# Dealing a block's slots out by 4 (rank mod 16) + rank div 16 in a one-core MoE kernel

## The chip, the core and the metric

The kernel runs as one program on one core of a Trainium2 chip. The metric is the device time in microseconds (us). In these texts TensorE is PE, VectorE is DVE, ScalarE is ACT, GpSimd is POOL and SyncE is SP. The core's transfers run on 16 DMA engines; SP's transfers are those of the hardware queue (q1), POOL's those of the software queue (q0).

## The reference

One decoder layer over 512 tokens of width 2048: a norm, an input projection, two recurrent branches, a merge, and then a mixture of experts, which alone matters here. Its core, shortened:

```python
g_sel = jnp.argmax(g_logits, axis=-1)                        # 1 of 4 groups
top_l, top_i = lax.top_k(e_logits, TOP_K_IN_GROUP)           # 2 of 8 experts in it
expert_id = g_sel[:, None] * EXPERTS_PER_GROUP + top_i       # 512 x 2 of 32 experts
...
def expert_block(args):
    xb, e = args
    return (jax.nn.silu(xb @ w_gate[e]) * (xb @ w_up[e])) @ w_down[e]
...
out = jax.ops.segment_sum(ys * buf_w[:, None], buf_tok, num_segments=n_tok + 1)[:n_tok]
```

Each expert has three weight matrices of 2048 x 512 floats (4 MB each). Each of the 1024 pairs of a token and an expert takes one row of 2048 floats (8 KB) in and gives one row of 8 KB out. In which order an expert's tokens stand in its block changes nothing in the sum.

## The kernel before

The program goes through the norm, the two branches and the merge, then the routing, the experts and the combination. The experts' stage is what the change touches. It is a loop over blocks of 64 slots (`SLOTS`), one block for each expert and more only where an expert has over 64 tokens. Blocks are taken in pairs: an even block's rows lie in partitions 0 to 63 of the tile `ex_x`, an odd block's in partitions 64 to 127; slot s of a block is partition s (or 64 + s). The outputs lie in the same way in the tile `y_rows`.

Routing. `phase_route` computes for each token and expert a rank, the number of that expert's tokens before this one. Two tables are then made by one-hot comparisons and matrix products: `of_slot` says which slot a token has in its block, `of_block` which block. The one-hot of the first block compares the rank with `slots` (L1750), the others compare the centred place in the block with `from_middle` (L1778):

```python
1750: mark("first", tt(of_first[:], rank_ps[:, 0:TT, 0:1].to_broadcast([P, TT, P]),
...
1778: order.done(tt(of_slot[:], wide(in_block, P), along(from_middle[:], P), ALU.is_equal))
```

`slots` and `from_middle` are two small constants that `route_consts` makes on DVE during the merge, from the ramp 0, 1, 2, ... A token of rank r gets the column in which the constant has r, so the slot is r before the change. The product gives `tok_table` (the token of slot s of block b) and `row_table` (the row of the output table to which slot s of block b goes). A slot without a token gets an index out of range, and the transfer skips it.

The loop. In each block POOL issues one indirect transfer that gathers the rows of the block after the next (L1953, `fetch`) and one that scatters the rows that this block made (L1972):

```python
1953: pool.indirect_dma_start(xg[s], None, io["hn"], bass.IndirectOffsetOnAxis(ap=rows, axis=0),
1972: pool.indirect_dma_start(io["ys"], bass.IndirectOffsetOnAxis(ap=y_idx[u][:], axis=0), y_sb[u], None,
```

SP loads the next expert's weights in 12 transfers of 1 MB, four of `w_gate` and four of `w_up` (L1515, L1516) and four of `w_down` (L1521), each as soon as PE has used what the buffer held (`unit_used`). There is one buffer for each piece, so SP can be at most 12 pieces, one expert, ahead of PE. PE multiplies the piece with the turned rows (L2046, L2048), turns the next block's rows (L2032), waits for the activation by ACT and DVE (L1985, L2010, L2013), turns that (L2059) and multiplies with `w_down` (L2068, L2070). ACT copies the result to `y_rows` (L1993). PE waits for each piece until all DMA engines that carry a part of it have delivered it. After the loop `phase_combine` reads the output table (L2101), adds it and normalises.

The router, computed on the reference's inputs, gives the 32 experts these numbers of tokens, in the order of the blocks: 20, 37, 24, 20, 40, 30, 44, 35, 33, 35, 38, 29, 22, 25, 38, 26, 26, 34, 29, 29, 28, 38, 35, 35, 45, 43, 21, 29, 37, 38, 36, 25. There are 32 blocks, and no block is full.

Of the kernel before, what the change touches and what calls it, by code (L numbers as in the profile page):

```python
# [16 lines left out]
ALU = mybir.AluOpType  # L17
# [23 lines left out]
SLOTS = 64  # L41
# [1281 lines left out]
def phase_merge(nc, io, keep, block, sems):  # L1323
# [8 lines left out]
    with ExitStack() as ctx:  # L1332
# [98 lines left out]
        @block.vector  # L1431
        def _(dve):
            dve.wait_ge(keep["rw_gate_stored"], keep["rw_gates"])
            with dve.Fori(0, half) as j:
                for q in range(2):
                    f = 2 * j + q
                    ring_used(dve, ring, BEFORE + f)
                    dve.wait_ge(gates_in[q], 16 * j + 16)
                    dve.tensor_tensor(part_h[:], z[q][0], gates[q][:, 0, :], ALU.mult)
                    dve.tensor_tensor(part_r[:], z[q][1], gates[q][:, 1, :], ALU.mult).then_inc(parts, 1)  # L1440
                    dve.wait_ge(parts, f + 1)
                    dve.tensor_tensor(merged[:], part_h[:], part_r[:], ALU.add).then_inc(sum_ready, 1)
                    ring_lo(dve, ring, merge_slot(q), BEFORE + f + 2)
                    dve.wait_ge(sum_hi, f + 1)
                    dve.tensor_tensor(one(m_lo, f), merged[:], one(m_hi, f).bitcast(F32), ALU.subtract).then_inc(sum_lo, 1)
            dve.wait_ge(parts, KT)
            dve.sem_inc(branches_done, 1)
            for j in range(N_OUT):
                if j == 2:
                    route_consts(dve, keep)  # L1450
                for kq in range(4 if j < N_OUT - 1 else 2):
                    f = KT + 4 * j + kq + 2
                    ring_lo(dve, ring, merge_slot(f), BEFORE + f)
                dve.wait_ge(x_in, 16 * TT)
                for t in range(TT):
                    dve.wait_ge(group_done, 4 * j + t + 1)
                    b = h[:, t, NB * j:NB * j + NB]
                    dve.tensor_tensor(b, banks[j % 2][t], b, ALU.add).then_inc(h_ready, 1)
# [77 lines left out]
def route_consts(dve, keep):  # L1536

    pre, made = keep["pre"], Order(dve, keep["const_made"], keep["params_made"])
    ramp, ident = keep["const"][:, CONST["ramp"], :], keep["const"][:, CONST["ident"], :]
    place, ts = ramp[:, P - 1:P], dve.tensor_scalar  # L1540
    n_logits = N_GROUPS + N_EXPERTS
    made.done(dve.tensor_tensor(pre["fold"][:], ident[:, 0:n_logits], ident[:, P // 2:P // 2 + n_logits], ALU.add))
    made.done(dve.memset(pre["ones_e"][:], 1.0))
    made.done(ts(pre["limits"][:], ramp[:, 0:PER_GROUP], float(SLOTS), None, ALU.mult))
    made.done(ts(pre["ramp_late"][:], ramp[:, 0:PER_GROUP], float(P), None, ALU.add))
    for s in range(2):
        made.done(ts(pre["from_middle"][:, SLOTS * s:SLOTS * s + SLOTS], ramp[:, 0:SLOTS], -(SLOTS - 1) / 2.0, None, ALU.add))
    for s in range(2):
        made.done(ts(pre["slots"][:, SLOTS * s:SLOTS * s + SLOTS], ramp[:, 0:SLOTS], 1.0, None, ALU.mult))
    made.done(ts(pre["expert_slot"][:], ramp[:, 0:N_EXPERTS], float(SLOTS), None, ALU.mult))  # L1550
    made.done(ts(pre["from_first"][:], ramp[:, 0:N_EXPERTS], float(SLOTS), -(SLOTS - 1) / 2.0, ALU.mult, ALU.add))
    made.done(ts(pre["evens"][:], ramp[:, 0:MAX_BLOCKS // 2], 2.0, None, ALU.mult))
    for n in range(2 * TT):
        made.done(ts(pre["value"][:, n:n + 1], place, float(T * (n // TT) + P * (n % TT) + 1), None, ALU.add))
    made.wait()
    made.done(dve.memset(pre["limits"][:, 0:1], float(4 * T)))

    row0 = ident[0:SLOTS, 0:1]
    made.done(ts(pre["empty"][:], row0, float(2 * T - NOWHERE), float(NOWHERE + 1), ALU.mult, ALU.add))
    made.done(ts(pre["no_token"][:], row0, float(T - NOWHERE), float(NOWHERE + 1), ALU.mult, ALU.add))  # L1560
    made.done(ts(pre["ceiling"][:], row0, float(2 * T - 1 - NOWHERE), float(NOWHERE), ALU.mult, ALU.add))
    made.wait()
    dve.wait_ge(keep["router_in"], 16 * 5)
    w = keep["par"][:, ROWS["norm_ffn"][0]:ROWS["norm_ffn"][0] + KT].rearrange("p (k a) -> p k a", a=1)
    dve.tensor_tensor(pre["w_router"][:], pre["w_router"][:], w.to_broadcast([P, KT, n_logits]),
                      ALU.mult).then_inc(keep["router_ready"], 1)
# [682 lines left out]
```

## Time and profile before

| | us |
|---|---|
| median of 3 runs | 2871.19 (2868.44 to 2871.45) |
| the profiled execution | 2868.37 |
| its span, first to last instruction | 2866.5 |
| PE busy | 2549.9 (89% of the span) |
| DVE busy | 922.2 (32%) |
| ACT busy | 779.4 (27%) |

The profiled execution lies 2.8 us below the median, and 1.9 us of it lie outside the span. The share of a DMA queue is given as a part of the time of all 16 DMA engines: 100% is 16 engines at work all the time, one engine alone is about 6%. The row "DMA share" of a stretch is the same for all queues together. A packet is counted where it starts, so that in stretches of under 1 us shares are rough and the counts of packets are what is to be read. Each row of 8 KB that is gathered or scattered is one packet of 8 KB; packets under 512 B are the 4-byte ones that end a transfer on each engine.

### The profile page before, as it was taken

The numbers are of one execution on the slowest core, as the hardware profiler recorded it, in microseconds if no ns is written. First come the engines' busy times: TensorE is split into PE (matmuls) and PEld (weight loads), VectorE is DVE, ScalarE is ACT, GpSimd is POOL, SyncE is SP. The second block draws the span as 40 slices with busy tenths as digits, with TensorE's granted clock in tenths as the row PEclk, the third lists the DMA queues.
The fourth block names the chain that finished last, engine by engine and source line by source line (L and its number), as shares of the span: only waits on it lengthen the run. The fifth ranks groups of instructions, "written<-read, shape, count | busy, mean of one in ns | idle before, by whom it ended". The sixth has DMA issues, their size and how long they took to land. (4 is left out here: it accounts for less than half of the span.)

```text
span 2866.5 us, 39233 instructions
## 1 busy us (share of the span) xinstructions
PE 2549.9 (89%) x15517; PEld 1679.3 (59%) x15517; DVE 922.2 (32%) x1288; ACT 779.4 (27%) x961; POOL 146.4 (5%) x232
## 2 busy tenths in 40 slices
PE   6999999999999999998899997987788777888882
PEld 5888888887777777776788775332333323333331
DVE  5333333335554555544444233100010000010004
ACT  5444444433433344333222221111111111111111
POOL 0000000000000000000000000000000000000000
PEclk9999999999999999999899998999999999999895
DMA  5333333332222222223555425999999999999994
GB/s 151 103 104 103 103 103 103 104 99 62 76 75 75 68 74 76 75 70 101 179 145 186 126 103 216 405 407 409 409 406 411 412 411 401 401 398 409 380 399 186
DMA packets 315851, 610.92 MB, mean 213 GB/s; under 512 B 18926, under 2 KB 240490, under 8 KB 261994
## 3 DMA queue, kind: packets, MB, share of 16 engines
q1 hardware_dynamic: 304092, 568.03, 54.9%
q0 software_dynamic: 11664, 41.45, 4.0%
q8 instruction: 80, 1.31, 0.2%
q14 instruction: 15, 0.12, 0.0%
HBM read 585.82 MB, written 41.42 MB: 219 GB/s over the span
## 5 line engine op out<-in xcount | busy, mean ns | idle before, releaser
L2046 PE MATMUL bank<-ex_w_gate,ex_xt_sb 128*64 128x512 f32 x1024 | 479.8, 618 | 163.0 <-DMA ex_w_up<-in_expert_w_up_dram 149.4
L153 PE MATMUL in_z<-xn_hi,in_hi 128*128 128x512 f32 x1456 | 584.1, 401 | 13.4 <-DVE in_lo L185 8.1
L153 PE MATMUL in_z<-xn_lo,in_hi 128*128 128x512 f32 x1456 | 582.8, 400 | 0.0
L153 PE MATMUL in_z<-xn_hi,in_lo 128*128 128x512 f32 x1456 | 579.6, 398 | 0.0
L2048 PE MATMUL bank<-ex_w_up,ex_xt_sb 128*64 128x512 f32 x1024 | 482.6, 620 | 0.0
L2046 PEld LDWEIGHTS bank<-ex_w_gate,ex_xt_sb 128*64 128x64 f32 x1024 | 136.8, 142 | 475.3 <-issue 475.1
L185 DVE TENSOR_TENSOR in_lo<-in_raw,in_hi 128x2048 fp32r<-128x2048 f32 x122 | 289.7, 2375 | 302.4 <-ACT in_hi L180 183.5
L2010 DVE SCALAR_TENSOR_TENSOR ex_sig_gate<-bank,rs_slot,ex_sig_gate 64x512 f32<-64x512 f32 x32 | 23.8, 744 | 924.4 <-ACT ex_sig_gate L1985 924.4
L153 PEld LDWEIGHTS in_z<-xn_hi,in_hi 128*128 128x128 f32 x1456 | 274.4, 188 | 76.2 <-DVE in_lo L185 8.7
L153 PEld LDWEIGHTS in_z<-xn_lo,in_hi 128*128 128x128 f32 x1456 | 274.4, 188 | 67.4 <-issue 10.8
L153 PEld LDWEIGHTS in_z<-xn_hi,in_lo 128*128 128x128 f32 x1456 | 274.1, 188 | 63.6 <-issue 5.0
L2068 PE MATMUL bank<-ex_w_down,ex_ht_sb 128*64 128x512 f32 x512 | 270.0, 688 | 25.5 <-ACT ex_ht_sb L1987 25.5
L2070 PE MATMUL bank<-ex_w_down,ex_ht_sb 128*64 128x512 f32 x512 | 270.1, 688 | 0.0
L180 ACT ACTIVATE in_hi<-in_raw 128x2048 fp32r<-128x2048 f32 x90 | 171.8, 1908 | 68.5 <-PE in_z L153 68.4
L2068 PEld LDWEIGHTS bank<-ex_w_down,ex_ht_sb 128*64 128x64 f32 x512 | 77.3, 157 | 189.2 <-issue 189.2
L1985 ACT ACTIVATE ex_sig_gate<-bank,rs_slot 64x512 f32<-64x512 f32 x32 | 21.8, 682 | 576.0 <-PE bank L2048 576.0
L1993 ACT ACTIVATE y_rows<-bank 64x512 f32<-64x512 f32 x128 | 75.8, 592 | 258.7 <-PE bank L2070 256.3
L2048 PEld LDWEIGHTS bank<-ex_w_up,ex_xt_sb 128*64 128x64 f32 x1024 | 136.8, 142 | 0.0
L1411 ACT ACTIVATE in_hi<-in_raw 128x2048 fp32r<-128x2048 f32 x30 | 57.6, 1919 | 241.0 <-PE mg_z_rw L145 123.1
L2032 PEld LDWEIGHTS bank<-const,ex_x 64*128 64x128 f32 x528 | 66.5, 220 | 26.8 <-issue 26.8
L2070 PEld LDWEIGHTS bank<-ex_w_down,ex_ht_sb 128*64 128x64 f32 x512 | 77.4, 157 | 0.0
L897 ACT ACTIVATE rw_x_tr<-rw_b 128x512 f32<-128x512 f32 x40 | 23.9, 598 | 194.5 <-PE rw_b L1203 194.5
(439 smaller groups left out, 2897.5 us busy)
## 6 DMA issues: line engine op xcount, KB each, us to landing
ex_w_gate<-in_expert_w_gate_dram SPq DMA_DIRECT2D x128, 1024.0 KB, 15.5
ex_w_up<-in_expert_w_up_dram SPq DMA_DIRECT2D x128, 1024.0 KB, 27.5
ex_w_down<-in_expert_w_down_dram SPq DMA_DIRECT2D x128, 1024.0 KB, 26.1
in_raw<-in_w_in_dram SPq DMA_DIRECT2D x91, 1024.0 KB, 5.7
in_raw<-in_w_out_dram SPq DMA_DIRECT2D x32, 512.0 KB, 4.7
in_raw<-in_w_branch_hg_dram SPq DMA_DIRECT2D x16, 512.0 KB, 5.0
in_raw<-in_w_branch_rw_dram SPq DMA_DIRECT2D x16, 512.0 KB, 6.1
mg_gates<-scratch_gate SPq DMA_DIRECT2D x16, 512.0 KB, 3.8
```

What stands on the lines that cost most here:

```text
L153: return pe.matmul(out, w[:, k, :], x[:, k, :], start=(n == 0), stop=(n == PASSES * KT - 1), skip_group_check=True)
L180: act.activation(ring["hi"][slot][:], ring["raw"][slot][:], ACT.Copy).then_inc(ring["hi_done"], 1)
L185: dve.tensor_tensor(ring["lo"][slot][:], ring["raw"][slot][:], ring["hi"][slot][:].bitcast(F32), ALU.subtract).then_inc(ring["lo_done"], 1)
L897: act.activation(x_tr[:], twin[0][:, 0, :].rearrange("p (q s) -> p q s", s=P), ACT.Copy).then_inc(x_ready, 1)
L1411: act.activation(ring["hi"][slot][:], ring["raw"][slot][:], ACT.Copy).then_inc(ring["hi_done"], 1)
L1993: act.activation(y_sb[u][:, f:f + D_EXPERT], down_ps[c][part, :], ACT.Copy).then_inc(y_read, 1)
L2010: dve.scalar_tensor_tensor(act_g[high, :], gate_up[low, :], rs[u][low, :], sig[low, :], ALU.mult, ALU.mult).then_inc(gated, 1)
L2032: mm = pe.transpose(x_ps[g][:, k, :], rows, (ident, ident_high)[s])
L2046: pe.matmul(gate_up[low, :], x_t[u][:, k, :], w_gate[n][:, j, :], start=first, stop=last, skip_group_check=True)
L2048: mm = pe.matmul(gate_up[high, :], x_t[u][:, k, :], w_up[n][:, j, :], start=first, stop=last, skip_group_check=True)
L2068: pe.matmul(down_ps[c][low, :], h_t[:, n, :], w_down[n][:, lo_c:lo_c + D_EXPERT], start=(n == 0), stop=(n == DC - 1), skip_group_check=True)
L2070: mm = pe.matmul(down_ps[c][high, :], h_t[:, n, :], w_down[n][:, hi_c:hi_c + D_EXPERT], start=(n == 0), stop=(n == DC - 1), skip_group_che ...
```

## The change

The constants `from_middle` and `slots` are written in another order. Place 4b + a of each 64 now holds 16a + b, with a from 0 to 3 and b from 0 to 15, so rank r stands at place 4 (r mod 16) + r div 16. Both constants hold two copies of 64 places, one for each half of the partitions, as before. Everything that reads them is as it was; no instruction is added, taken out or moved, and four instructions on DVE have other access patterns.

```diff
+    spread = lambda a, how: a.rearrange(how, a=SLOTS // 16)
...
     for s in range(2):
-        made.done(ts(pre["from_middle"][:, SLOTS * s:SLOTS * s + SLOTS], ramp[:, 0:SLOTS], -(SLOTS - 1) / 2.0, None, ALU.add))
+        made.done(ts(spread(pre["from_middle"][:, SLOTS * s:SLOTS * s + SLOTS], "p (b a) -> p b a"), spread(ramp[:, 0:SLOTS], "p (a b) -> p b a"),
+                     -(SLOTS - 1) / 2.0, None, ALU.add))
     for s in range(2):
-        made.done(ts(pre["slots"][:, SLOTS * s:SLOTS * s + SLOTS], ramp[:, 0:SLOTS], 1.0, None, ALU.mult))
+        made.done(ts(spread(pre["slots"][:, SLOTS * s:SLOTS * s + SLOTS], "p (b a) -> p b a"), spread(ramp[:, 0:SLOTS], "p (a b) -> p b a"),
+                     1.0, None, ALU.mult))
```

The first 16 tokens of an expert now stand in slots 0, 4, 8, ..., 60, the next 16 in slots 1, 5, 9, ..., 61, and the 33rd to the 48th in slots 2, 6, ..., 62. Before, 32 tokens filled slots 0 to 31 and left 32 to 63 empty.

## Rows read from the trace of the kernel before

**Rows 1.** The page: slices of the span, DMA share and rate.

```profile
PE   6999999999999999998899997987788777888882
PEclk9999999999999999999899998999999999999895
DMA  5333333332222222223555425999999999999994
GB/s 151 103 104 103 103 103 103 104 99 62 76 75 75 68 74 76 75 70 101 179 145 186 126 103 216 405 407 409 409 406 411 412 411 401 401 398 409 380 399 186
```

**Rows 2.** Waits of PE, 1850 to 2790 us: us in total, times, longest.

```profile
PE bank L2046 <- DMA ex_w_up<-in_expert_w_up_dram: 146.9, 81, 4.2
PE bank L2068 <- ACT ex_ht_sb L1987: 23.1, 29, 0.8
PE bank L2059 <- DVE ex_h L2013: 10.2, 29, 0.4
PE bank L2046 <- PE bank L2070: 9.0, 14, 0.9
```

**Rows 3.** The line of ACT's sigmoid, once a block: durations, starts.

```profile
L1985 ACT ACTIVATE ex_sig_gate<-bank,rs_slot x32: 682/682/683, 1800.1 to 2801.9; 64x512 f32<-64x512 f32 x32
```

**Rows 4.** Timeline, the first products of the stage: start, duration, idle before, releaser.

```profile
1784.74 1.09 PE L2046 MATMUL bank<-ex_w_gate,ex_xt_sb 128*64 128x512 f32 x1 [3.25 <-DVE ex_xt_sb L2001]
1784.75 1.11 PE L2048 MATMUL bank<-ex_w_up,ex_xt_sb 128*64 128x512 f32 x1
```

**Rows 5.** Windows of the experts' stage: busy time by engine, clock, DMA share, rate.

```profile
2000.00:2100.00 100.00, 79.44 (x368) 31.68 (x370) 8.83 (x15) 14.28 (x23) 7.72 (x13) 0.97 1.01 408
2200.00:2300.00 100.00, 77.98 (x356) 30.59 (x354) 8.83 (x15) 12.86 (x20) 6.79 (x12) 0.95 1.01 411
2600.00:2700.00 100.00, 81.42 (x354) 31.77 (x352) 8.83 (x15) 12.87 (x20) 5.64 (x10) 0.90 0.98 387
2700.00:2800.00 100.00, 83.11 (x363) 32.34 (x361) 8.84 (x15) 11.59 (x19) 7.95 (x14) 0.91 0.94 382
```

**Rows 6.** Windows of the last block, columns as above.

```profile
2780.00:2790.00 10.00, 9.48 (x45) 3.24 (x42) 0.00 (x0) 2.37 (x4) 0.93 (x1) 1.00 1.01 421
2791.00:2794.00 3.00, 0.88 (x5) 0.40 (x6) 0.00 (x0) 0.00 (x0) 0.38 (x2) 1.00 0.31 128
2794.00:2797.00 3.00, 3.00 (x11) 1.08 (x9) 0.00 (x0) 0.00 (x0) 0.96 (x2) 0.58 0.15 60
2797.00:2800.00 3.00, 3.00 (x15) 1.13 (x13) 0.00 (x0) 0.00 (x0) 0.00 (x0) 0.85 0.13 52
2802.00:2804.00 2.00, 1.99 (x16) 1.85 (x16) 1.31 (x2) 0.62 (x1) 0.00 (x0) 1.00 0.06 25
2806.00:2808.00 2.00, 2.00 (x6) 0.49 (x4) 0.00 (x0) 0.00 (x0) 0.00 (x0) 0.50 0.05 20
2808.00:2810.00 2.00, 2.00 (x8) 0.57 (x6) 0.00 (x0) 0.00 (x0) 0.00 (x0) 0.50 0.00 0
```

**Rows 7.** DMA packets, 2819.6 to 2819.85 us and 2820.1 to 2820.5 us.

```profile
DMA packets 22, 0.11 MB, mean 426 GB/s; under 512 B 9, under 2 KB 9, under 8 KB 9
...
DMA packets 14, 0.10 MB, mean 246 GB/s; under 512 B 2, under 2 KB 2, under 8 KB 2
```

**Rows 8.** DMA packets and queues, 2818 to 2823 us, the last scatter.

```profile
DMA packets 81, 0.21 MB, mean 43 GB/s; under 512 B 55, under 2 KB 55, under 8 KB 55
...
q0 software_dynamic: 80, 0.21, 19.4%
```

**Rows 9.** DMA packets and queues, 2022 to 2027 us, weights alone.

```profile
DMA packets 290, 2.11 MB, mean 423 GB/s; under 512 B 32, under 2 KB 32, under 8 KB 32
...
q1 hardware_dynamic: 290, 2.11, 101.5%
```

**Rows 10.** The same, 2006 to 2010 us, a scatter beside weights.

```profile
DMA packets 258, 1.68 MB, mean 420 GB/s; under 512 B 53, under 2 KB 53, under 8 KB 53
...
q1 hardware_dynamic: 178, 1.32, 78.5%
q0 software_dynamic: 80, 0.36, 21.9%
```

**Rows 11.** The same, 2015 to 2020 us, a gather beside weights.

```profile
DMA packets 266, 1.61 MB, mean 323 GB/s; under 512 B 69, under 2 KB 69, under 8 KB 69
...
q1 hardware_dynamic: 186, 1.33, 80.0%
q0 software_dynamic: 80, 0.29, 21.6%
```

**Rows 12.** DMA packets around three more gathers, from 1827, 2305, 2732 us, 5 us each.

```profile
DMA packets 279, 1.62 MB, mean 324 GB/s; under 512 B 81, under 2 KB 81, under 8 KB 81
...
DMA packets 287, 1.75 MB, mean 349 GB/s; under 512 B 74, under 2 KB 74, under 8 KB 74
...
DMA packets 273, 1.63 MB, mean 326 GB/s; under 512 B 74, under 2 KB 74, under 8 KB 74
```

**Rows 13.** The lines L1547 and L1549, which write the constants.

```profile
L1547 DVE TENSOR_SCALAR rt_from_middle<-const x2: 193/193/193, 1655.4 to 1655.5; 128x64 f32<-128x64 f32 x2
...
L1549 DVE TENSOR_SCALAR rt_slots<-const x2: 193/194/194, 1655.6 to 1655.7; 128x64 f32<-128x64 f32 x2
```

## The prediction

> **What bounds the kernel now.** I read the page's slices first. From slice 25 to 39 the DMA engines are at 9 tenths or more and move about 400 GB/s, where before they moved 60 to 220 [rows 1]. This is the experts' stage, and it lasts from about 1785 us [rows 4] to about 2817 us. The windows sharpen it: 408 to 411 GB/s with a DMA share of 1.01, while PE is busy 80 of 100 us; from 2600 us on the share falls to 0.98 and 0.94 and the rate with it [rows 5]. The waits of PE say what it lacks: 146.9 us for the weights, 42 us for all others together [rows 2]. So the stage is bound by transfers, one block in (2801.9 - 1800.1) / 31 = 32.3 us [rows 3].
>
> PE needs every piece from all 16 engines, so the stage runs at the pace of the engine with the most to do. The last block shows which that is. Until 2790 us all 16 are busy; then the share is 0.31, 0.15, 0.13, and from 2802 us to 2808 us it is 0.06, which is one engine of 16 [rows 6]. One engine is some 17 us behind the crowd, a second some 11, a third some 4. The weights are the same for all engines, so what differs is the rows.
>
> **Who carries which slot.** The last scatter runs with nothing beside it. It moves 0.21 MB, 25 rows of 8 KB [rows 8]. In its first quarter of a microsecond 22 - 9 = 13 large packets start, and after a pause 14 - 2 = 12 more [rows 7]. So 13 engines had the 25 rows: twelve had two, one had one. That is a deal in pairs: slots 0 and 1 to one engine, 2 and 3 to the next, sixteen engines for slots 0 to 31. By ones it would have been 16 and 9, by fours 7 engines in four waves. I take it that slots 32, 33 come back to the first engine, 34, 35 to the second and so on. With the numbers of tokens of the 32 blocks, the engines then have these rows, once in the gathers and once in the scatters: 97, 90, 82, 72, 70, 69, 65, 64, 64, 64, 59, 56, 52, 46, 40, 34.
>
> A packet of 8 KB costs an engine 0.315 us: with weights alone 101.5% of 16 x 5 us is 81.2 us for 290 - 32 = 258 large packets [rows 9]. A scatter's row beside weights costs the same, 21.9% of 64 us for 44 rows, 0.32 us [rows 10]. So the first engine should end 7 x 2 x 0.315 = 4.4 us behind the second, 9.5 behind the third and 15.8 behind the fourth. The trace has about 6, 13 and 17 [rows 6]. By fours five engines would be last together, with 128 rows each; by ones five would end within 6 us. Only the pairs leave one engine alone.
>
> The whole of the first engine's work adds up too. From 1785 to 2808 us, 1023 us, it moves 31 experts of 96 packets (12 MB in 8 KB packets over 16 engines), 937 us; about 188 rows, 59 us; and it is slowed in the gathers. In the 5 us around a gather the rate is 323, 324, 349 and 326 GB/s [rows 11, 12] where it is 423 with weights alone [rows 9], so (423 - 330.5) / 423 x 5 = 1.1 us are lost per engine, 34 us in 31 gathers. The sum is 1030. It is never idle.
>
> **The change, part by part.**
>
> The four instructions on DVE: 0.193 us each, at 1655 us [rows 13], in the merge, where PE is the busy engine and DVE waits. The other access pattern can cost nothing or, if each took twice as long, 0.8 us; I take 0, and 0.8 if the cover were gone. The comparisons that read the constants keep their size.
>
> The rows. Rank r goes to slot 4 (r mod 16) + r div 16. Ranks 0 to 31 fill slots 4b and 4b + 1. Those two slots are one pair, number 2b, and pairs go to engines by their number mod 16: always an even engine, and b and b + 8 the same one. A block with 32 tokens gives eight engines four rows each and the others none. Only ranks from 32 on reach the odd engines. Summed over the 32 blocks: 123, 20, 121, 19, 119, 18, 119, 13, 116, 11, 111, 8, 109, 4, 109, 4. The largest load rises from 97 to 123, by 26 rows in the gathers and 26 in the scatters: 52 x 0.315 = **+16.4 us**. Nothing hides it, since this engine has no idle time.
>
> The slowing in the gathers. The last scatter shows its source: 19.4% of 80 us for 25 rows is 0.62 us each [rows 8], twice the 0.32 beside weights. There all twelve engines with two rows worked without a pause, and each pair of engines read four neighbouring partitions; beside weights an engine alternates between a row and a weight. So two engines at work on the same few partitions halve each other. In a gather before, each four partitions get rows from two engines and weights from a third. After, they get rows from one engine, but for four rows instead of two, and weights from one that in half of the cases has no rows of its own and never pauses. From below: no slowing, -34 us. From above: each engine with twice the rows loses twice the time, +34 us. I take the place between from one packet: each of four rows waits for one weight packet of another engine, 4 x 0.315 = 1.26 us for 1.1 now, **+5 us** in 31 gathers.
>
> The Trainium skill bears on this (SBUF — State Buffer, section "Door 1: The DMA port swizzle"): four neighbouring partitions share a port for transfers with the four that lie 32 further on, and 64 partitions reach 8 of 16 ports. The trace agrees as far as the 0.62 us go. By this rule the rows per port hardly change, and a sum made by ports alone would be near 0 instead of +21.
>
> The last scatter: 4 x 0.32 us on one engine with its partitions to itself, for 2 x 0.62 now: nothing. The early gathers: PE's first turn stands behind the table's products, nothing.
>
> Sum: 16.4 + 5 = +21 on the profiled 2868.4 gives 2890. The median lies 2.8 higher, so 2892; I say **2891 us**.
>
> **Rivals.**
>
> *The slots from 32 on come back shifted by an odd number of engines.* The trace does not show which engines get the pairs from 32 on, only that they add to full ones; a shift of one also leaves one engine alone. Then b and b + 8 lie on engines of both kinds, and the largest load is 76 rows for 97: 42 x 0.315 = -13 us, and perhaps some of the 34 us, **2853**, faster. It speaks against this that a transfer's halves of 32 would have to be treated differently. It decides from the first block on: the last engines would end nearly together.
>
> *The relief cancels the load.* If a gather's slowing falls by half (one engine with rows per four partitions, not two), -17 + 16.4 is about 0: **2871**.
>
> *The slowing grows.* Four rows and the four weights between them all wait: 2.5 us per gather, +1.4 x 31 = +44, with the rows +60, **2930**. For it: the eight engines share all gathers. Against it: the weights between go to other partitions, at least in part.
>
> *Fours.* If slot div 4 were the engine, the largest load would fall from 128 rows to 81: -94 x 0.315 = -30, **2841**, the one case in which the new order evens the load. The 13 first packets of the last scatter speak against it [rows 7]. The Trainium skill (DMA: Bandwidth & Descriptors, section "Why a DMA increments its semaphore by 16 and not by 1") lets one transfer be cut into 16 equal shares of its partitions, which for 64 would be such fours. The trace disagrees.
>
> **How the numbers follow.** The forecast has 0.76, with a range of its own of 2877 to 2912: the 16.4 us with a slowing between -10 and +25. The relief 0.10, the growth beyond 2912 0.05, the shift 0.07, fours 0.02. A measurement of this kernel tells about 0.2%, 5.7 us, from no change. Faster: the shift, fours and a little of the relief, 0.10. The same: most of the relief and the lowest end of the forecast, 0.10. Slower: 0.80. The range takes in the relief's middle: 2871 to 2912.
>
> **What would show it.** In the last block the share should stand near 0.5 (eight engines) for some microseconds, where it fell to 0.31 and 0.06; in the last scatter some 8 or 9 packets start in the first wave and each takes near 0.32 us; PE's wait for weights in the stage rises from 147 us by about 20; the time per block goes from 32.3 to about 33.0 us; the experts' stage moves the same bytes at some 2% less. The rate around a gather tells the second term. I am wrong if the largest load is not on eight even engines, which the last block's shares would show at once, or if the engines are slowed by less in the gathers than now.

## The result and the profile after

The changed kernel takes 2889.22 us in the median (2887.79 to 2890.73, 4 runs) against 2869.82 (2867.38 to 2871.45, 4 runs) for the kernel before: 19.4 us more, ratio 1.0068 with a 95% interval of 1.0051 to 1.0086. The profiled execution took 2888.68 us, its span 2886.9 us.

The rates of the page's slices answer to [rows 1]. The stages up to slice 23 are nearly as they were; the experts' stage moves the same bytes at a lower rate, often under 400 GB/s.

```profile
GB/s 154 105 102 102 102 102 102 102 97 76 67 70 91 65 73 73 66 88 136 137 151 187 125 79 278 409 406 400 399 393 386 404 395 379 394 390 397 379 397 210
```

The line of the sigmoid (now L1988) gives the time of a block, as in [rows 3]: (2823.6 - 1801.8) / 31 = 32.96 us, where it was 32.3. That is 20 us over 31 blocks, so the whole difference is in this loop. The forecast was 2891 us, with a range of 2871 to 2912.

```profile
L1988 ACT ACTIVATE ex_sig_gate<-bank,rs_slot x32: 682/682/683, 1801.8 to 2823.6; 64x512 f32<-64x512 f32 x32
```

The windows of the last block (columns as in [rows 6]: busy time by engine, clock, DMA share, rate) show who is late. The share stands at 0.51 and 0.50 for four microseconds, which is eight engines of 16, and then goes down in steps until 2830 us. Before, it was 0.31 in the first microseconds and ended with one engine.

```profile
2816.00:2818.00 2.00, 2.00 (x12) 0.69 (x8) 0.00 (x0) 0.00 (x0) 0.98 (x2) 1.00 0.51 209
2818.00:2820.00 2.00, 0.72 (x6) 0.15 (x4) 0.00 (x0) 0.00 (x0) 0.00 (x0) 1.00 0.50 209
...
2824.00:2826.00 2.00, 1.65 (x15) 1.54 (x15) 1.65 (x3) 0.25 (x1) 0.00 (x0) 1.00 0.30 127
...
2828.00:2830.00 2.00, 2.00 (x6) 0.52 (x5) 0.00 (x0) 0.00 (x0) 0.00 (x0) 0.50 0.07 29
```

The packets of the last scatter, first from 2839.9 to 2840.15 us and then from 2838.5 to 2843.5 us, answer to [rows 7, 8].

```profile
DMA packets 28, 0.07 MB, mean 262 GB/s; under 512 B 20, under 2 KB 20, under 8 KB 20
...
q0 software_dynamic: 80, 0.21, 10.3%
```

In the first wave 28 - 20 = 8 rows start, where it was 13: eight engines have the 25 rows. And the share of the same 80 packets is 10.3% of 80 us for 19.4%, so a row costs 0.33 us for 0.62. Each engine now has its four partitions to itself. The 80 packets are 25 rows and 55 small ones, and 55 is 16 ends and 39 more, one for each of the 39 slots without a token: the small packets are not only the ends of a transfer.

The waits of PE: in the window of [rows 2] the wait for the weights went from 146.9 to 151.0 us. That window holds fewer blocks after than before, so I compare the same 31 blocks, from the first sigmoid to the last: first before, then after.

```profile
PE bank L2046 <- DMA ex_w_up<-in_expert_w_up_dram: 149.4, 82, 4.2
...
1800.10:2801.90 1001.80, 806.49 (x3597) 317.20 (x3597) 91.28 (x155) 125.69 (x201) 70.17 (x124) 0.93 1.00 402
```

```profile
PE bank L2049 <- DMA ex_w_up<-in_expert_w_up_dram: 154.8, 78, 4.2
...
1801.80:2823.60 1021.80, 820.05 (x3597) 320.76 (x3598) 91.19 (x155) 125.56 (x202) 69.94 (x124) 0.92 0.99 393
```

The loop is 20.0 us longer. The wait has 5.4 us of it and PE's busy time 13.6, with a granted clock of 0.92 for 0.93 (by these two rounded figures, an estimate of 9 of the 13.6 us). One could take the clock for the cause. The run with half the groups (below) speaks against it: its loop is 41.0 us longer at a clock of 0.93, PE is as busy as before, and the wait has all of it.

```profile
PE bank L2051 <- DMA ex_w_up<-in_expert_w_up_dram: 191.4, 86, 5.8
...
1800.50:2843.30 1042.80, 807.56 (x3597) 317.19 (x3598) 91.22 (x155) 125.57 (x202) 69.96 (x124) 0.93 0.99 385
```

Two executions of that same kernel took 2908.07 us at a clock of 0.950 and 2908.87 us at 0.958. So a lower clock moves time from PE's wait to PE's work in this loop, and does not set how long the loop is. The wait alone would have hidden most of the loss.

### The profile page after: what moved, and what is told of

It is laid out like the page before. It is cut to its first block and busy times, and to the rows that moved or that the text cites. A ratio compares the mean times of both kernels' runs of the same rounds, so it can differ in the third digit from the quotient of the medians.

```text
span 2886.9 us, 39233 instructions
## 1 busy us (share of the span) xinstructions
PE 2563.4 (89%) x15517; PEld 1684.5 (58%) x15517; DVE 921.9 (32%) x1288; ACT 779.1 (27%) x961; POOL 146.1 (5%) x232
## 5 line engine op out<-in xcount | busy, mean ns | idle before, releaser
L2049 PE MATMUL bank<-ex_w_gate,ex_xt_sb 128*64 128x512 f32 x1024 | 486.8, 625 | 169.6 <-DMA ex_w_up<-in_expert_w_up_dram 154.8
L2051 PE MATMUL bank<-ex_w_up,ex_xt_sb 128*64 128x512 f32 x1024 | 489.4, 628 | 0.0
L2071 PE MATMUL bank<-ex_w_down,ex_ht_sb 128*64 128x512 f32 x512 | 275.7, 700 | 25.6 <-ACT ex_ht_sb L1990 25.6
L2073 PE MATMUL bank<-ex_w_down,ex_ht_sb 128*64 128x512 f32 x512 | 275.8, 701 | 0.0
L1988 ACT ACTIVATE ex_sig_gate<-bank,rs_slot 64x512 f32<-64x512 f32 x32 | 21.8, 682 | 589.4 <-PE bank L2051 589.4
```

The source lines that it names most:

```text
L2049: pe.matmul(gate_up[low, :], x_t[u][:, k, :], w_gate[n][:, j, :], start=first, stop=last, skip_group_check=True)
L2051: mm = pe.matmul(gate_up[high, :], x_t[u][:, k, :], w_up[n][:, j, :], start=first, stop=last, skip_group_check=True)
L2071: pe.matmul(down_ps[c][low, :], h_t[:, n, :], w_down[n][:, lo_c:lo_c + D_EXPERT], start=(n == 0), stop=(n == DC - 1), skip_group_check=True)
L2073: mm = pe.matmul(down_ps[c][high, :], h_t[:, n, :], w_down[n][:, hi_c:hi_c + D_EXPERT], start=(n == 0), stop=(n == DC - 1), skip_group_che ...
```

## The experiments

The theory (A) is that the stage runs at the pace of the DMA engine with the largest sum of rows, pairs of slots by engine, at 0.63 us for a row that is gathered and scattered. The main rival (B) is that a transfer is slow because its own rows crowd on few engines. A second term (C) is the slowing in gathers by rows that go to the same partitions. All ratios are to the kernel before, measured on the same chip; the chips of the groups of runs differ.

For each deal A counts the largest sum over the 32 blocks that one engine has. B can be counted too: in each block the most rows that any engine has, and the sum of that. B's count is 97 before and reversed, 123 in the changed kernel and with half the groups, 81 for the even pairs and the folded deal. Mirroring the odd blocks does not change it. So without mirroring A and B give the same numbers in all but the folded deal, and only the mirrored and the folded deals part them. Some of the expectations below take B for less than that, "no change" where its count falls from 97 to 81.

**Reversed slots.** Rank r to slot 63 - r. The line of `slots` is changed in the same way.

```diff
-ts(pre["from_middle"][...], ramp[:, 0:SLOTS], -(SLOTS - 1) / 2.0, None, ALU.add)
+ts(pre["from_middle"][...], ramp[:, 0:SLOTS], -1.0, (SLOTS - 1) / 2.0, ALU.mult, ALU.add)
```

> Rank r goes to slot 63 - r: the used slots are now the upper ones, the pairs land on the engines in mirrored order, and the largest load stays 97 rows. Theory A (the stage runs at the pace of the engine with the most rows, pairs of slots per engine, 0.63 us for a row that is gathered and scattered): no change, 2869.8, within 3 us. Theory B (what costs is that one transfer's rows lie on fewer engines): also no change, 16 engines as before. Theory C (the low partitions are special, so any other place costs): slower by some us.

Measured: 2873.55 us, ratio 1.0009 (1.0000 to 1.0018). That is 0 to 5 us more. The largest sum is the same 97, and so is the time but for these few us. They may be the slowing in the gathers: the rate around a gather (explained under "Half the groups") is 312 GB/s here for 330 before, by which 6 us would be expected. Why the rate is lower with the upper slots is not shown.

**Even pairs.** Of 32 neighbouring ranks each engine gets two, 16 apart, and the ranks from 32 on go to one engine each. The line of `from_middle` is changed in the same way.

```diff
+    pairs_of = lambda a, how: a.rearrange(how, h=2, l=2)
-        made.done(ts(pre["slots"][...], ramp[:, 0:SLOTS], 1.0, None, ALU.mult))
+        made.done(ts(pairs_of(pre["slots"][...], "p (h b l) -> p h b l"),
+                     pairs_of(ramp[:, 0:SLOTS], "p (h l b) -> p h b l"), 1.0, None, ALU.mult))
```

> Rank r goes to slot 2 (r mod 16) + (r div 16) mod 2 + 32 (r div 32), so that engine r mod 16 gets it; each transfer uses 16 engines as before, and the largest load falls from 97 to 81 rows. Theory A: 16 x 0.63 = 10 us less, 2860. Theory B (rows of one transfer on few engines): no change, 2870, since blocks of up to 32 tokens have two rows per engine at most in both. If slots were dealt to the engines in fours or by ones, the time would not follow the 81.

Measured: 2856.61 us, ratio 0.9946 (0.9933 to 0.9960), 14 us less than before where A says 10. This does not speak against B: in 16 of the 17 blocks with over 32 tokens the first engine had four rows and now has at most three, and B's count falls from 97 to 81 as well. The last block's windows have no single late engine: the share is 0.56 from 2785 us on, and 0.12 from 2795 us on, which is two engines.

```profile
2795.00:2800.00 5.00, 3.83 (x23) 1.62 (x24) 1.95 (x4) 0.38 (x1) 0.00 (x0) 1.00 0.12 49
```

**Half the groups.** The loads of the changed kernel, on engines whose slots lie in four of the eight groups of partitions. In the code two bits of the slot's number change places against the changed kernel; the lines of `from_middle` are changed in the same way.

```diff
+    part_of = lambda a, s, n: a[:, SLOTS * s:SLOTS * s + SLOTS].rearrange("p (c x y l) -> p c x y l", c=8, x=2, y=2)[:, :, n // 2, :, n % 2]
+        for n in range(4):
+            made.done(ts(part_of(pre["slots"], s, n), ramp[:, 16 * n:16 * n + 16].rearrange("p (c y) -> p c y", y=2),
+                         1.0, None, ALU.mult))
```

> The engine loads of the changed kernel (123 at most, eight engines with four rows in a full 32), but on engines 0, 1, 4, 5, 8, 9, 12, 13, so that a gather writes only four of the eight groups of four partitions (244 rows in the fullest group for 143 in the changed kernel and 187 in the kernel before). Theory A alone: as the changed kernel, 2889. Theory A with the slowing of two engines on the same partitions: slower than the changed kernel, by some 1 to 2 us per gather in 31 gathers at most, 2900 to 2940. If the partitions don't matter: 2889.

Measured: 2908.47 us, ratio 1.0131 (1.0115 to 1.0146), 19 us more than the changed kernel with the same loads and the same crowding within a transfer. So loads alone are not all; C is real. The packets in the 5 us from the start of the same gather (35 rows) show it, first in the changed kernel (from 2017.9 us), then with half the groups (from 2020.2 us); before, it was 323 GB/s [rows 11].

```profile
DMA packets 248, 1.52 MB, mean 303 GB/s; under 512 B 63, under 2 KB 63, under 8 KB 63
```

```profile
DMA packets 201, 1.16 MB, mean 231 GB/s; under 512 B 60, under 2 KB 60, under 8 KB 60
```

I read such a window for 29 gathers of each kernel, from 0.1 us ahead of the gather's first row. The mean rate is 329.6 GB/s before, 315.3 after and 252.9 with half the groups. Against 423 that is a loss of 1.10, 1.27 and 2.01 us per gather. From the changed kernel to half the groups it is 0.74 x 31 = 23 us; 19 were measured. The 29 windows of a kernel scatter, so that a mean rate has a standard error of 3 to 4.5 GB/s: the 0.17 us between the kernel before and the changed one are known to 0.06 or so, the 0.74 are far beyond that.

The last scatter, with nothing beside it, shows the same without weights. Here too eight engines have the 25 rows, but two of them read in one group of partitions. From 2858.4 to 2863.4 us:

```profile
q0 software_dynamic: 80, 0.21, 19.8%
```

That is 0.63 us for a row, where eight engines on eight groups took 0.33. So the 0.62 us of the kernel before come from two engines in one group, and not from how many engines are at work.

**The changed kernel, odd blocks mirrored.** Six small instructions turn the place in the block around where the block's number is odd.

```diff
+        step(ts(flip[:], at_block[:], 0.5, -0.25, ALU.mult, ALU.add))
+        step(ts(flip[:], flip[:], float(3 << 22), None, ALU.add))
+        step(ts(flip[:], flip[:], -float(3 << 22), None, ALU.add))
+        step(stt(flip[:], flip[:], -2.0, at_block[:], ALU.mult, ALU.add))
+        step(ts(flip[:], flip[:], -2.0, 1.0, ALU.mult, ALU.add))
+        step(tt(in_block[:], in_block[:], flip[:], ALU.mult))
```

> The changed kernel, but in blocks of odd number the slots are mirrored (six small DVE instructions more on the routing path, about 1.2 us). Each transfer still lies on eight engines with four rows each in a full 32, but the eight are the even ones in one block and the odd ones in the next, so the largest sum is 68 rows for 123. Theory A: 55 x 0.63 = 35 us less than the changed kernel, 29 x 0.63 = 18 us less than the kernel before, with the 1.2 us 2853. Theory B (what costs is the crowding within one transfer): as the changed kernel, 2890.

Measured: 2860.70 us, ratio 0.9965 (0.9952 to 0.9979): 28.5 us less than the changed kernel and 10 less than before. This refutes B, which has 123 here as in the changed kernel. Each transfer is as crowded, eight engines with four rows, and the loss is gone, since a late engine is another one in the next block. The gain over the kernel before falls short of A's 18. The rate around a gather is 312 GB/s, as low as in the changed kernel, and that costs 6 us against the kernel before; with it and the 1.2 us some 11 are left, and 10 were measured. From 2700 to 2780 us all 16 engines are at work:

```profile
2700.00:2780.00 80.00, 66.67 (x297) 26.07 (x295) 8.83 (x15) 11.02 (x19) 5.46 (x9) 0.91 1.01 413
```

**The kernel before, odd blocks mirrored** (the same six lines).

> The kernel before (two rows per engine in slots 0 to 31), with the slots of odd blocks mirrored as in the run before: largest sum 68 rows. Theory A: 29 x 0.63 = 18 us less than before, and 1.2 us for the six small instructions, 2853. If the crowding of one transfer on eight engines has a price of its own, this is faster than the changed kernel with mirrored odd blocks (2860.7), which has the same largest sum, by that price; if it has none, the same 2861.

Measured: 2862.51 us, ratio 0.9967 (0.9955 to 0.9979). The same as the one above, with the same largest sum of 68, although its transfers use 16 engines. B has 97 here for 123 there, 16 us apart, and is refuted again. A price of 6 us, which the rates around the gathers would give (329 GB/s here for 312 above), does not show in this pair, but each of the two times is known to about 4 us only. Here 9 us were gained where A says 18, and the rate in the gathers, as before, does not explain it.

**Even pairs, odd blocks mirrored.**

> Both improvements together: slot 2 (r mod 16) + (r div 16) mod 2 + 32 (r div 32), mirrored in odd blocks. Largest sum 67 rows, average 64. Theory A: 14 x 0.63 = 9 us less than the even pairs alone (2856.6), plus 1.2: 2849. If the stage is no longer bound by one engine but by PE or by all engines together, it stays at about 2855.

Measured: 2857.01 us, ratio 0.9953 (0.9939 to 0.9967): no better than the even pairs alone, where A says 8 us better with the 1.2. The rate around a gather is 333 GB/s, so this is not the gathers' slowing either. The next three runs ask why.

**Folded.** Ranks from 32 on in mirrored order, no instruction on the routing path; the lines of `from_middle` are changed in the same way.

```diff
+        lane = lambda n, l: pre[n][:, SLOTS * s:SLOTS * s + SLOTS].rearrange("p (h b l) -> p h b l", h=2, l=2)[:, :, :, l]
+        for l in range(2):
+            made.done(ts(lane("slots", l)[:, 0], ramp[:, 16 * l:16 * l + 16], 0.0, None, ALU.add))
+            made.done(ts(lane("slots", l)[:, 1], ramp[:, 16 - 16 * l:32 - 16 * l], -1.0, SLOTS - 1.0, ALU.mult, ALU.add))
```

> Ranks 0 to 31 as in the even pairs (engine r mod 16), ranks from 32 on in mirrored order (engine 15 - r mod 16), by four more small instructions in the merge and none on the routing path. Largest sum 66 rows of an average of 64, for 81 with the even pairs. If the busiest engine still sets the pace below 81 rows: 15 x 0.63 = 9 us less than the even pairs, 2848. If, as the mirrored odd blocks let one think, all engines together are the bound by then: 2856, as the even pairs.

Measured: 2850.66 us, ratio 0.9923 (0.9910 to 0.9937), the fastest version: 20.7 us less than before, 6 less than the even pairs. By A it is 31 x 0.63 = 19.5. B has 81 here as for the even pairs and would give the same time as they had. So the busiest engine still sets the pace below 81 rows.

**The six instructions alone**, with the factor held at 1, once with the folded deal and once with the kernel before.

```diff
-        step(ts(flip[:], flip[:], -2.0, 1.0, ALU.mult, ALU.add))
+        step(ts(flip[:], flip[:], 0.0, 1.0, ALU.mult, ALU.add))
```

> The folded deal (2850.7) with the six small instructions of the mirrored variants, but with a factor that is always 1, so that nothing is mirrored. The mirrored even pairs, with nearly the same largest sum (67 for 66), took 2857. If the 6 us between them are the price of the six instructions: 2857. If the six cost what they show in the trace, about 1.2 us: 2852, and the rest belongs to the mirroring itself.

> The kernel before with the same six instructions and nothing mirrored: 1.2 us more than before, 2872, if the six cost what they show; 2877 if they cost 6 us.

Measured: 2850.68 us, ratio 0.9925 (0.9911 to 0.9939), and 2874.05 us, ratio 1.0011 (1.0002 to 1.0020). Nothing with the folded deal, 1 to 6 us with the kernel before: on both sides of the 1.2 expected. With the folded deal they do not explain the 6 us by which the mirrored even pairs fall short of it. So where odd blocks are mirrored on top of a deal that uses all 16 engines, 4 to 8 us of A's gain are missing, and why stays open.

**No gathers.** A bound of 0 in `fetch` lets only the first token's row through, so the experts' inputs are left out.

```diff
-                                    bounds_check=T - 1, oob_is_err=False).then_inc(x_in[s], 16)
+                                    bounds_check=0, oob_is_err=False).then_inc(x_in[s], 16)
```

> The kernel before with a bound of 0 in the gathers, so that no token's row but the first is gathered: this leaves out the experts' inputs. Rows are only scattered: the busiest engine loses 97 x 0.315 = 31 us and the slowing in the gathers, 34 us. Theory: 2870 - 65 = 2805, or somewhat more if PE then bounds some blocks. If the slowing is not caused by the gathers, 2839.

> The changed kernel with the same bound, so again only scatters: 26 rows more on the busiest engine, once. Theory: 26 x 0.315 = 8.2 us more than the kernel before with the same bound, nothing else, since scatters are not slowed beside weights. If more than about 12 us, the scatters have a slowing too; if near 0, the engines are no longer the bound without gathers.

> The half-groups kernel (eight engines with four rows, on four of the eight groups of four partitions) with a bound of 0 in the gathers, which leaves out the experts' inputs. If the 19 us that it takes beyond the changed kernel come from gathers that write the same partitions: as the changed kernel without gathers, 2821, within 3 us. If scatters that read the same partitions are slowed too: 2825 to 2835.

Measured: 2809.85 us, ratio 0.9778 (0.9761 to 0.9794); 2821.09 us, ratio 0.9820 (0.9803 to 0.9838); 2816.80 us, ratio 0.9808 (0.9794 to 0.9821). The gathers' rows and their slowing cost the kernel before 61 us, for 65 expected. Windows of 100 us of the first two, the kernel before and then the changed kernel, have nearly the 423 GB/s of weights alone [rows 9], so scatters slow nothing:

```profile
2000.00:2100.00 100.00, 86.46 (x382) 34.38 (x378) 9.61 (x17) 13.53 (x21) 6.77 (x12) 0.90 1.01 421
```

```profile
2000.00:2100.00 100.00, 82.55 (x370) 32.30 (x367) 8.83 (x15) 13.00 (x21) 7.94 (x14) 0.93 1.01 422
```

The changed deal costs 11.2 us in the medians of the scatters alone (9.7 us in the spans, 2818.3 and 2808.6), for 8.2 expected; each of the two ratios is known to about 5 us. And half the groups cost nothing beyond the changed deal without gathers (-4 us), where they cost 19 with them. So the slowing belongs to the gathers, whose rows are written to the same partitions, and not to the scatters, whose rows are read from them beside weights.

## Why the prediction was right

The forecast was slower, 2891 us; 2889.22 were measured. Its mechanism, one engine's rows, is what the runs show. That it came within 2 us is in part luck, as the two terms below tell.

The bound. The stage runs at the pace of the engine with the largest sum of rows. The table has the differences in the median from the kernel before. "By rows" is 0.63 us for each row more or less; "by both" adds the slowing in 31 gathers by the mean rate around a gather (before: 330 GB/s), read in the same way for each kernel.

| deal | largest sum | rate around a gather | by rows | by both | measured |
|---|---|---|---|---|---|
| changed, half the groups | 123 | 253 | +16 | +44 | +38 |
| changed | 123 | 315 | +16 | +22 | +19 |
| reversed | 97 | 312 | 0 | +6 | +3 |
| even pairs | 81 | 329 | -10 | -10 | -14 |
| changed, mirrored | 68 | 312 | -18 | -12 | -10 |
| before, mirrored | 68 | 329 | -18 | -18 | -9 |
| even pairs, mirrored | 67 | 333 | -19 | -20 | -14 |
| folded | 66 | 330 | -20 | -20 | -21 |

The mirrored deals have their six instructions on top, some 1.2 us. By both, five of the eight come out within 4 us. The others are half the groups, 6 us of 38, and the two mirrored deals that use all 16 engines, 9 and 6 us; these two stay unexplained.

The deal in pairs, with slots from 32 on coming back to the same engines: confirmed by the eight engines of the last block, the 8 first packets of the last scatter and the times in the table. The rival with a shift and the rival by fours are refuted by the same rows: by either of them the 25 rows would have started on 16 engines. The prediction says that the trace disagrees with the rule of the Trainium skill named there (DMA: Bandwidth & Descriptors, section "Why a DMA increments its semaphore by 16 and not by 1"). That goes too far. The rule gives how many engines share a transfer, 16 for 64 partitions, and in the deal in pairs too each of 16 engines has four slots; that the four are neighbours was the prediction's own addition, and it is this that the trace refutes.

The first term, +16.4 us: its half for the scatters was 8.2 and came out at 11.2 or 9.7 us.

The second term, +5 us: the loss per gather went from 1.10 to 1.27 us, where the prediction had 1.1 and 1.26, so 0.17 x 31 = 5 us, known to 2 us or so. The reason that was given, two engines at work on the same few partitions, is borne out by half the groups and by the last scatters. That the 5 us are a part of the 19 is not shown by a run of its own. What the gathers cost in all is 19.4 - 11.2 = 8.2 us, where the prediction has 8.2 for the rows and 5 for the slowing, 13.2. The scatters came out 3 us high and the gathers 5 us low, both within what these runs can tell, and in the sum the two nearly cancel. The rate is a mean over all 16 engines; that the busiest ones lost the same was not measured.

The sentence that the rows per port hardly change is wrong. Counted over the 32 blocks, the fullest group of partitions has 187 rows before and 143 after, so a sum by the fullest port alone would have foretold a gain, and not nothing. The loads decide first, then the ports. The Trainium skill (SBUF — State Buffer, section "Door 1: The DMA port swizzle") makes a transfer's bandwidth depend on how many ports its partitions reach, and the trace agrees: with half of the groups in use a gather lost 2.01 us for 1.27.

DVE's four instructions (now L1548 and L1551) cost 0.208 and about 0.206 us for 0.193 [rows 13], hidden.

What was foreseen wrongly is one sign to look for, not a term of the sum: PE's wait for weights was to rise by about 20 us and rose by 5.4 over the same blocks, because PE's own work became slower by 13.6 us.

## What to carry to other kernels

Where a loop is bound by transfers, look at its last microseconds: the DMA share in steps of 1/16 says how many engines are late and by how much, and rows that seem spread within each transfer can still load the same engine in all of them. Deal the used rows so that the sums over the whole loop are even, not only those of one transfer; crowding that moves from engine to engine cost much less (10 us under the kernel before, where the same crowding on fixed engines cost 19). Find the deal from the trace (how many packets start in the first wave) before writing a permutation for it: here an order that evens a deal in fours was slower by 0.7% on a deal in pairs, and an order made for the pairs was faster by 0.8%.

## What was not expected of the hardware

An indirect transfer of 64 rows gives slots 2e, 2e + 1, 32 + 2e and 33 + 2e to the same engine e: 13 engines start on the 25 rows of slots 0 to 24, and 8 engines when the same rows lie in slots 0, 4, 8, ... A slot without an index moves no row (39 of the last scatter's 55 small packets are such slots), and no other row takes its place, so that half-filled blocks load the engines unevenly. A row of 8 KB takes 0.33 us where an engine has its group of four partitions to itself and 0.62 us where two engines read in one group at once, 0.63 us also with eight engines only. But beside weights a scatter has no such slowing (421 GB/s of 423), and a gather does (330, 315 and 253 GB/s).
